# A hybrid attention, scan and expert layer on one core: slot tables by one-hot matmuls, and a reordered beginning and end

## What is computed

```python
h = rms_norm(x, mix_norm_w)
proj = h @ w_in                       # q, k, v, z, xBC, dt, gate_a, gate_s
...                                   # 8-head differential attention, Mamba-2 scan
dt = softplus(dt_raw + dt_bias)       # step sizes of the scan's 32 heads
x = x + (sigmoid(gate_a) * (A @ W_A) + sigmoid(gate_s) * (B @ W_B)) @ w_out
tok = rms_norm(x, moe_norm_w)
logits = tok @ router_w + router_b
top_vals, top_idx = top_k(logits, 4)  # of 32 experts
gate = softmax(top_vals)
...                                   # sort token choices by expert, clamped SwiGLU expert, sum with gates
x = x + sigmoid(rms_norm(x, ple_norm_w) @ w_ple_gate) * (p @ w_ple_proj)
y = rms_norm(x, final_norm_w)
```

## Time and profile before

| | |
|---|---|
| median of three runs | 2371.75 us (2371.46 to 2371.77) |
| the profiled execution | 2371.01 us, its span 2369.3 us |
| TensorE busy | 2126.9 us, 90% of the span |
| VectorE, ScalarE, GpSimd busy | 70%, 53%, 9% |
| mean granted TensorE clock | 0.957 of full speed |
| moved by DMA | 527.68 MB, mean 223 GB/s |
| expert loop | from 1089 to 2268 us |

### The profile page before, as it was taken

The page is one execution under the profiler, slowest core; times in us unless marked ns, Lnnn a source line. Parts: engine busy times, 40 slices in busy tenths (PEclk is TensorE's granted clock), DMA queues, the critical chain, the costliest instruction groups (busy, mean ns, idle before and its releaser), DMA issues.

```text
span 2369.3 us, 30053 instructions
## 1 busy us (share of the span) xinstructions
PE 2126.9 (90%) x9452; PEld 1634.0 (69%) x9452; DVE 1649.7 (70%) x1797; ACT 1248.5 (53%) x1419; POOL 202.5 (9%) x141
## 2 busy tenths in 40 slices
PE   4999799879769999955999999999999999999967
PEld 3777677768645555434877878778778787787746
DVE  4676756668451111135999999999999999999955
ACT  3444243332310010013787777777877777787744
POOL 0000000101000000021021110111101111110020
PEclk9999899989879999967999999999999999999989
DMA  3225222112023222065999999999999999999672
GB/s 97 77 55 195 55 80 63 51 38 71 18 92 104 78 55 62 29 231 181 356 364 389 367 369 382 366 385 374 359 387 370 370 383 366 384 370 365 242 244 87
DMA packets 244019, 527.68 MB, mean 223 GB/s; under 512 B 19830, under 2 KB 127942, under 8 KB 243974
## 3 DMA queue, kind: packets, MB, share of 16 engines
q1 hardware_dynamic: 228688, 481.73, 56.4%
q0 software_dynamic: 7424, 25.19, 3.0%
q10 hardware_dynamic: 7862, 20.19, 2.1%
HBM read 497.55 MB, written 29.49 MB: 222 GB/s over the span
## 4 chain that ended last, share of the span: by engine, by line
PE 70%; DVE 14%; issue 8%; ACT 4%; DMA 2%; ACTq 0%; SPq 0%; DVEq 0%; POOL 0%; POOLq 0%
PE psum L1621 66%; DVE h_lo L1491 4%; ACT h_hi L941 1%; DVE w_lo L1486 1%; PE psum L1901 1%; DVE arena L1506 1%; DVE arena L1189 1%; DVE arena L1509 1%; DVE arena L1516 1%; DVE residual L1564 1%; PE psum L1788 1%; PE psum L1741 1%; DMA arena<-in_final_norm_w 1%; PE psum L1628 1%; DMA arena<-in_lambda_k 0%
## 5 line engine op out<-in xcount | busy, mean ns | idle before, releaser
L1491 DVE TENSOR_TENSOR h_lo<-arena,h_hi 128x1024 fp32r<-128x1024 f32 x768 | 912.0, 1222 | 90.8 <-ACT h_hi L941 54.2
L941 ACT ACTIVATE h_hi<-arena 128x1024 fp32r<-128x1024 f32 x768 | 801.0, 1059 | 219.4 <-PE psum L1621 200.2
L1621 PE MATMUL psum<-h_hi,w_hi 128*128 128x512 f32 x2176 | 870.1, 400 | 20.2 <-DVE h_lo L1491 12.9
L1621 PE MATMUL psum<-h_hi,w_lo 128*128 128x512 f32 x2176 | 850.2, 391 | 0.0
L1621 PE MATMUL psum<-h_lo,w_hi 128*128 128x512 f32 x2176 | 850.2, 391 | 0.0
L1621 PEld LDWEIGHTS psum<-h_hi,w_hi 128*128 128x128 f32 x2176 | 410.9, 189 | 124.7 <-DVE h_lo L1491 26.0
L1621 PEld LDWEIGHTS psum<-h_hi,w_lo 128*128 128x128 f32 x2176 | 410.1, 188 | 87.4
L1621 PEld LDWEIGHTS psum<-h_lo,w_hi 128*128 128x128 f32 x2176 | 411.0, 189 | 84.9 <-issue 3.8
L1621 PE MATMUL psum<-arena 128*128 128x512 f32 (+7 forms) x1232 | 358.3, 459 | 39.5 <-DVE arena L1383 13.4
L1621 PEld LDWEIGHTS psum<-arena 128*128 128x128 f32 (+1 forms) x1232 | 188.4, 198 | 196.4 <-issue 153.8
L1055 DVE TENSOR_TENSOR w_lo<-arena,w_hi 128x1024 fp32r<-128x1024 f32 x80 | 100.5, 1257 | 131.1 <-ACT w_hi L744 130.9
(11 more groups left out here) (264 smaller groups left out, 1547.3 us busy)
## 6 DMA issues: line engine op xcount, KB each, us to landing
arena<-in_w_up SPq DMA_DIRECT2D x512, 512.0 KB, 7.3
arena<-in_w_down SPq DMA_DIRECT2D x256, 512.0 KB, 6.3
arena<-in_w_in SPq DMA_DIRECT2D x80, 512.0 KB, 3.9
y_dram<-arena ACTq DMA_DIRECT2D x32, 512.0 KB, 8.4
arena<-in_w_ssd_branch SPq DMA_DIRECT2D x8, 1024.0 KB, 5.6
y_dram<-arena SPq DMA_DIRECT2D x1, 7680.0 KB, 23.1
arena<-in_w_attn_branch SPq DMA_DIRECT2D x8, 512.0 KB, 3.7
arena<-in_w_out SPq DMA_DIRECT2D x2, 2048.0 KB, 13.3
```

Source lines behind the costliest of these rows:

```text
L941: act.activation(piece_hi[slot], rows, ACT.Copy).then_inc(piece_hi_ready, 1)
L1491: dve.tensor_tensor(piece_lo[slot], rows, piece_hi[slot].bitcast(F32), ALU.subtract).then_inc(piece_lo_ready, 1)
L1621: return pe.matmul(o, l, r, start=start, stop=stop)
```

## The change

1. **Beginning.** The mix norm weights are loaded whole, broadcast over partitions, behind x's first tile, and multiplied in with the scaling (as the router's norm does); the three norm vectors leave the parameter loads, twelve of which remain. The turned tile stays in PSUM, even and odd tiles in two pairs of banks, and both halves are split from there. ScalarE makes a dummy Sqrt before its first Square. The parameters are turned behind the dt projection, the bias loads are issued behind the split of the first two units.
2. **dt steps.** The dt result is turned behind head 0's q unit; `ask_dt` stands before VectorE's split of the third unit and `finish_dt` behind it, ScalarE's Exp calls behind its own part of that split.
3. **Biases.** Their split stands behind VectorE's part of the last head and before its `take_output`; the six stores stand behind ScalarE's last head.
4. **Slot tables.** The scatter, the DRAM table, its reload and its turn are gone. A row number is taken apart in block and place; for each choice VectorE writes a one-hot of its place (128 wide) and, 47 wide each, the token number and the gate at its block. Sixteen matmuls sum them to both tables. The first two gathers read their tokens straight from the table. The control numbers (`ended`, `owner`, `control`) stand behind the tables.
5. **End.** p and its projection go to buffers that come free earlier and are loaded ahead of the norm weights, TensorE waits for them alone, the final weights are loaded once the norm weights have landed. `add_ple` of a tile stands before `end_tile` of the one before.

```diff
+                if t == 0:
+                    sp.dma_start(mix_w, mix_norm_w[0].partition_broadcast(P)).then_inc(mix_w_landed, 16)
...
-            sp.wait_ge(slots_stored, 16 * TT * TOPK)
-            sp.dma_start(slot_rows[0:BLOCKS], slots_dram.rearrange("(b s) two -> b s two", s=P)
-                         ).then_inc(slot_rows_landed, 16)
...
-            sp.dma_start(ple_w, ple_norm_w[0].partition_broadcast(P)).then_inc(ple_in_landed, 16)
+            sp.dma_start(p_sb, p_d.rearrange("(t p) n -> p t n", p=P)).then_inc(ple_in_landed, 16)
+            for k in range(2):
+                sp.dma_start(w_pp[k], w_ple_proj[0, k * P:(k + 1) * P, :]).then_inc(ple_in_landed, 16)
             wait_down_lo(sp, EXPERTS - 1, DOWN_PIECES - 1)
...
-            sp.dma_start(p_sb, p_d.rearrange("(t p) n -> p t n", p=P)).then_inc(ple_in_landed, 16)
-            sp.dma_start(w_pp, w_ple_proj[0].rearrange("(k p) n -> p k n", p=P)).then_inc(ple_in_landed, 16)
-            sp.dma_start(final_w, final_norm_w.partition_broadcast(P)).then_inc(ple_in_landed, 16)
+            sp.dma_start(ple_w, ple_norm_w[0].partition_broadcast(P)).then_inc(ple_w_landed, 16)
+            sp.wait_ge(ple_w_landed, 16)
+            sp.dma_start(final_w, final_norm_w.partition_broadcast(P)).then_inc(ple_w_landed, 16)
...
-            pool.wait_ge(slots_zeroed, 16)
-            pool.wait_ge(slots_ready, 1)
-            for j in range(TT * TOPK):
-                pool.indirect_dma_start(slots_dram, bass.IndirectOffsetOnAxis(rows_u[:, j:j + 1], 0),
-                                        slot_info[:, j, :], None).then_inc(slots_stored, 16)
+            pool.wait_ge(logits_read, TT)
+            pool.iota(iota_slot, [[1, P]], base=0, channel_multiplier=0,
+                      allow_small_or_imprecise_dtypes=True).then_inc(iota_ready, 1)
             def fetch(b):
                 wait(pool, xg_landed, 16 * b)
-                pool.tensor_copy(block_token[:], slot_token[:, ds(b, 1)]).then_inc(block_token_ready, 1)
-                pool.wait_ge(block_token_ready, b + 1)
-                wait(pool, x_turned, b)
+                if isinstance(b, int) and b < 2:
+                    wait(pool, x_turned, b)
+                    token = slot_token[:, b:b + 1]
+                else:
+                    pool.tensor_copy(block_token[:], slot_token[:, ds(b, 1)]).then_inc(block_token_ready, 1)
+                    pool.wait_ge(block_token_ready, b - 1)
+                    wait(pool, x_turned, b)
+                    token = block_token[:]
                 pool.sem_inc(gather_cleared, 1)
-                pool.indirect_dma_start(xg, None, h2_dram, bass.IndirectOffsetOnAxis(block_token[:], 0)
+                pool.indirect_dma_start(xg, None, h2_dram, bass.IndirectOffsetOnAxis(token, 0)
...
-            for src in (mix_norm_w[0], moe_norm_w[0], ple_norm_w[0], ssd_norm_w[0], da_head_norm_w[0], conv_b[0]):
+            for src in (ssd_norm_w[0], da_head_norm_w[0], conv_b[0]):
...
+            own.mark(act.activation(small[:, 0:1], eps[:], ACT.Sqrt))
+            def split_h(t):
+                act.wait_ge(xn_turned, t + 1)
+                act.activation(h_hi[:, :, t * P:(t + 1) * P],
+                               psum[:, (4 - 2 * (t % 2)) * 512:(6 - 2 * (t % 2)) * 512].rearrange("p (k t) -> p k t", t=P),
+                               ACT.Copy).then_inc(h_hi_ready, 1)
...
+            for t in range(TT):
+                root_mean(0, t, xs[:, t, :], lambda: act.wait_ge(x_landed[t], 16), D, square_dump)
+                if t:
+                    split_h(t - 1)
+            split_h(TT - 1)
+            act.wait_ge(w_dt_landed, 16)
+            act.activation(wdt_hi[:], w_dt, ACT.Copy).then_inc(wdt_split, 1)
+            split(Unit(0))
+            split(Unit(1))
+            act.dma_start(bias_src[:, 0:512], b_up[0].rearrange("e n -> (e n)").rearrange("(p n) -> p n", p=P)
+                          ).then_inc(biases_landed, 16)
...
+                if first:
+                    act.wait_ge(lam_asked, 1)
+                    act.activation(lam[:, 2:4], lam[:, 0:2], ACT.Exp).then_inc(lam_exp_ready, 1)
+                    own.mark(act.activation(byhead[:, 1, :], byhead[:, 1, :], ACT.Exp))
+                    act.wait_ge(dt_exp_asked, 1)
+                    act.activation(dt_work[:, 2, :], dt_work[:, 1, :], ACT.Exp).then_inc(dt_exp_ready, 1)
...
+            act.wait_ge(bias_parts_ready, 1)
+            for i in range(3):
+                act.dma_start(bup_dram[i].rearrange("(p n) -> p n", p=P), bias_part[:, i, 0:512]
+                              ).then_inc(bias_stored, 16)
...
+                landed, weights = ((mix_w_landed, mix_w), (moe_w_landed, moe_w), (ple_w_landed, ple_w))[stage]
+                dve.wait_ge(landed, 16)
+                dve.scalar_tensor_tensor(out=buf[t % 2], in0=xs[:, t, :], scalar=stat[:, n, 0:1],
+                                         in1=weights, op0=ALU.mult, op1=ALU.mult).then_inc(xn_ready, 1)
...
+            def split_h(t):
+                dve.wait_ge(h_hi_ready, t + 1)
+                cols = slice(t * P, (t + 1) * P)
+                dve.tensor_tensor(h_lo[:, :, cols],
+                                  psum[:, (4 - 2 * (t % 2)) * 512:(6 - 2 * (t % 2)) * 512].rearrange("p (k t) -> p k t", t=P),
+                                  h_hi[:, :, cols].bitcast(F32), ALU.subtract).then_inc(h_lo_ready, 1)
+            for t in range(TT):
+                normalize(0, t, xn)
+                if t:
+                    split_h(t - 1)
+            split_h(TT - 1)
+            dve.wait_ge(wdt_split, 1)
+            dve.tensor_tensor(wdt_lo[:], w_dt, wdt_hi[:].bitcast(F32), ALU.subtract).then_inc(wdt_split, 1)
+            split(Unit(0))
+            split(Unit(1))
+            dve.wait_ge(dt_projected, 1)
+            dve.tensor_copy(dtT, bank(6)[0:SH]).then_inc(dtt_copied, 1)
...
-            attention(0)
+            attention(0, first=True)
...
             attention(HEADS - 1)
+            dve.wait_ge(biases_landed, 32)
+            own.then(dve.tensor_copy(bias_part[:, 0, :], bias_src))
+            own.then(dve.tensor_tensor(bias_rest, bias_src, bias_part[:, 0, :], ALU.subtract))
+            own.then(dve.tensor_copy(bias_part[:, 1, :], bias_rest))
+            own.then(dve.tensor_tensor(bias_rest, bias_rest, bias_part[:, 1, :], ALU.subtract))
+            dve.tensor_copy(bias_part[:, 2, :], bias_rest).then_inc(bias_parts_ready, 1)
...
+            dve.wait_ge(top_exp_ready, 1)
+            own.then(dve.tensor_reduce(top_sum[:, 0:TT], top_exp, AX, ALU.add))
+            own.then(dve.reciprocal(top_sum[:, 4:4 + TT], top_sum[:, 0:TT]))
+            own.mark(dve.tensor_tensor(gate_of, top_exp,
+                                       top_sum[:, 4:4 + TT].unsqueeze(2).broadcast_to([P, TT, TOPK]), ALU.mult))
...
+            own.then(dve.tensor_copy(rows_u[:], row_f))
+            own.then(dve.tensor_scalar(slot_u, rows_u[:], P - 1, None, ALU.bitwise_and))
+            own.then(dve.tensor_copy(slot_f, slot_u))
+            own.then(dve.tensor_tensor(block_f, row_f, slot_f, ALU.subtract))
+            by_block = [P, TT * TOPK, BLOCKS]
+            own.then(dve.tensor_tensor(block_hot[:, :, 0, :], iota_block[:].unsqueeze(1).broadcast_to(by_block),
+                                       block_f.unsqueeze(2).broadcast_to(by_block), ALU.is_equal))
+            own.mark(dve.tensor_tensor(block_hot[:, :, 1, :], block_hot[:, :, 0, :],
+                                       gate_of.rearrange("p t k -> p (t k)").unsqueeze(2).broadcast_to(by_block), ALU.mult))
+            own.wait()
+            for t in range(TT):
+                own.mark(dve.tensor_scalar(block_hot[:, t * TOPK:(t + 1) * TOPK, 0, :],
+                                           block_hot[:, t * TOPK:(t + 1) * TOPK, 0, :], token_id[:, t:t + 1], None,
+                                           ALU.mult))
+            for b in range(2):
+                dve.wait_ge(h2_stored[b], 16 * TT // 2)
+            dve.wait_ge(iota_ready, 1)
+            own.wait()
+            for t in range(TT):
+                by_slot = [P, TOPK, P]
+                dve.tensor_tensor(slot_hot[:, t * TOPK:(t + 1) * TOPK, :], iota_slot.unsqueeze(1).broadcast_to(by_slot),
+                                  slot_f[:, t * TOPK:(t + 1) * TOPK].unsqueeze(2).broadcast_to(by_slot), ALU.is_equal
+                                  ).then_inc(slots_ready, 1)
+            dve.wait_ge(slots_summed, 1)
+            own.mark(dve.tensor_copy(slot_token[:], bank(6, BLOCKS)))
+            own.wait()
+            dve.tensor_copy(gate_tab[:], bank(6, BLOCKS, BLOCKS)).then_inc(tables_ready, 1)
...
             add_ple(0)
             ple_split(3)
+            add_ple(1)
+            dve.wait_ge(ple_w_landed, 32)
             end_tile(0)
-            add_ple(1)
+            add_ple(2)
             end_tile(1)
-            add_ple(2)
+            add_ple(3)
             end_tile(2)
-            add_ple(3)
             end_tile(3)
...
```

(44 more changed lines are left out.)

213 lines of the change are left out of this document (74 added, 139 removed).

## The result

| | before | after |
|---|---|---|
| median of the runs shown with the result | 2371.6 us | 2329.4 us (2325.0 to 2331.1) |
| ratio to before, 95% interval | | 0.982 (0.981 to 0.983) |
| profiled execution, its span | 2371.0, 2369.3 us | 2325.0, 2323.2 us |
| mean granted clock of the span | 0.957 | 0.962 |

The forecast was 2330.9 us. Five more runs of the changed kernel, beside other runs of before, gave 2329.7 (2324.5 to 2331.8), ratio 0.982 (0.981 to 0.984). Runs of one kernel lie up to 7 us apart, so a difference of medians is good to some 2 us; where less is asked, the place in the trace decides. The runs of before beside each group of experiments had medians of 2369.5 to 2372.3 us, so experiments of different groups (1 to 4, 5 to 8, 9 to 11, 12) can differ by some 2 us for that reason too.

A forecast was written before the change was run, and what follows sets the result against it. TensorE, busy 90% of the span, was taken as the bound, so only its standstills could give time. -14.5 - 19.4 - 2.8 - 4.1 = -40.8 us from the median 2371.75 gave 2330.9 us, range 2324 to 2339.

The forecast's parts named there:

- Beginning: Start to head 0's scores: shorter ScalarE queue, earlier dt projection, clock level held; -14.5 us, bounds -11.7 to -16.
- Bias split: Five VectorE steps and six ScalarE issues fit in waits at the last head: 0; without that cover 3.75 us.
- Router: Row numbers to the first gather's landing, tables summed by matmuls instead of scatters: -19.4 us, bounds -13.5 to -22.5.
- rival (a): Router: 62 further columns add 3.3 us to the passes and the gather takes 8 us; 2336 us, chance 0.11.
- The row that I set against it: Profile row of 512-column passes at 0.43 us each, said to leave no room for a weight load beside the columns.
- Rival (e): Router: the first expert waits for something else, VectorE's low halves or weights; 2350 us, chance 0.03.
- Loop: Expert 0's first matmul to expert 31's last keeps its length, within 2 us of 1179; costed at nothing.
- End: Loads behind the last expert: turns of p and the adds come earlier, -2.8 us, bounds -1.5 and -4.
- rival (c): End gives nothing before its last steps, gathers or gate-weight split being late anyway; 2333.7 us, chance 0.07.
- Tail: Last output steps: the last tile's sum no longer waits for the output of tile 2; -4.1 us.
- Rival (b): Beginning gains 2.8 us less: ScalarE's issues still end at 9.3, first unit starts slow; 2333.7 us, chance 0.10.
- Rival (d): Granted clock falls in the expert loop, at 150 us of it 2360 us; chance 0.03, 0.02 of it slower than before.

The follow-up runs named there:

- experiment 1: Changed kernel with the router's slot tables made as before, by sixteen GpSimd scatters, reload and turns: 2347.6 us.
- experiment 3: Changed kernel with the last output steps in the old order, output step of a tile before the sum of the next: 2333.8 us.
- experiment 4: Changed kernel with p and its projection loaded behind the norm weights and TensorE waiting for all five loads, as before: 2331.8 us.
- experiment 10: Changed kernel without ScalarE's dummy Sqrt ahead of the first Square: 2329.3 us.
- experiment 2: Changed kernel with the two bias loads issued ahead of the first Square again: 2331.6 us.
- experiment 12: Kernel of experiment 9 with the twelve small parameter loads issued by SyncE behind x, dt weights and two units, not by ScalarE: 2321.8 us, ratio 0.979.
- experiment 11: Changed kernel with VectorE's five bias steps behind the copy of the last head's output instead of ahead: 2331.7 us.
- experiment 8: Changed kernel with thirteen of the sixteen table matmuls 376 columns wide instead of 94: 2332.3 us.
- experiment 7: Changed kernel with the control numbers made beside the table sums instead of behind the tables: 2332.1 us.
- experiment 5: Changed kernel run again unaltered, for its spread: 2329.7 us.
- experiment 6: Changed kernel with tables made tile by tile and four low halves of the gate weights ahead of the copy of p: 2326.8 us, ratio 0.981.
- experiment 9: Changed kernel with tables made tile by tile, and p and its projection issued ahead of the gate weights: 2325.5 us, ratio 0.981.

## Why the prediction was right, and where its steps were off

**Beginning**, -14.5 taken, -16.2 at head 0's scores, -15.5 at the row numbers; the medians leave it 17.6 (41.9 less the 17.9, 4.2 and 2.2 of experiments 1, 3 and 4). The steps named came as laid out: the removed second table load (experiment 10), the 4 us that VectorE's order holds tile 2, the level held from the dt projection on, the dt turns behind unit 0. The cover of the dt step chain held: it ended at 46.9 and kT was copied by 47.5, 4 us ahead of the scores. The term mis-sized is ScalarE's queue. I kept the last issues at what they took before, ending near 8.0; they ended at 6.93 (experiment 2: an issue behind fewer loads is 0.5, not 1.4 to 2.2). The mix weights ahead of x cost nothing at that start; at the earlier start of experiment 12 x's tiles are what is late.

**Bias split**, 0, and 3.75 without its cover: 0 (the shift is the same 15.5 us on both sides of it) and 3.65 (experiment 11).

**Router**, -19.4 taken, -20.9 in the trace, -20.15 and -17.9 by undoing it. The tables stood 12.9 us behind the start of the row numbers' sum: block tables 0.94 each for 0.98, passes 7.11 for 7.1, so rival (a) was out by the first trace. The row that I set against it held, but the clock beside it was 1.00 and not 0.50 (experiment 8): a column costs half as much there. The sentence of the Trainium skill on weight loads (TensorE: Matmul & The Clock Gate) stands there under The mechanism; the traces disagree with it, as these passes take what their columns take, with nothing for the load. The term mis-sized is the gather, 4.29 for 6.0. I had seen that the control numbers put off the next weights, and took only half of it: the gather is then alone, and beside them it is 7.34 (experiment 7). Rival (e) didn't come.

**Loop**, 0: 1179.2 to 1178.6, but this is luck, from two parts that nearly cancel. TensorE ran expert 0's first matmuls at the 1.2 GHz level for 2.7 us, before 5.7, and its first two rounds took 69.2 us for 71.4; the last expert gave 1.7 back (experiment 5).

**End**, -2.8 taken for the loads, -4.5 to the first add in the trace, 4.3 by undoing it in the trace and 2.2 in the medians. p was turned 7.1 us behind the last matmul, where I had 8 to 9; the other traces with this order of loads have 7.7 to 10.0. Of rival (c) a part is true: the fourth add waited 0.43 us for its gather, and with the low halves earlier the gathers are the bound (experiment 6). **Tail**, -4.1 taken, -4.2 measured and 4.2 by undoing it.

**Rival (b)** had the issues end late: they ended early. **Rival (d)**: the loop kept its clock at 1.00.

**The spread.** Those first two rounds are of two kinds: 69.2 to 69.4 us in six of the fourteen traces (both of the changed kernel, experiments 1, 2, 7, 8) and 70.8 to 71.7 in the other eight, and what differs is how soon the clock rises in expert 0. The stretch where it begins, in the changed kernel and in experiment 3:

```profile
1050.00:1060.00 10.00, 7.63 (x28) 5.95 (x27) 4.10 (x4) 4.43 (x5) 1.98 (x2) 0.72 0.65 217
```

```profile
1050.00:1060.00 10.00, 7.59 (x21) 6.03 (x22) 3.31 (x3) 2.21 (x3) 1.27 (x2) 0.50 0.67 234
```

Seven matmuls fewer in the same busy time. That is 2.4 us of the 7 that runs of one kernel differ by, and no step of mine had it as a chance. The quick runs also have the higher clock: of the nine runs of the changed kernel the three under 2327 us have a mean granted clock of 0.962 or 0.963, the six others 0.959 to 0.961. What stays open: why the clock rises early in some executions, the rest of the spread, and why the medians of experiments 1, 4, 10 and 11 show 1.6 to 2.2 us less than their traces. The changed kernel was traced twice, in executions of 2325.0 and 2326.1 us, both with the short rounds; those near 2330 have no trace.

## What to carry to other kernels

Ahead of a first instruction, count an engine's DMA issues at what they cost in a short queue as well as in the long one, and ask whether they must stand there at all: moving twelve small loads to another queue gave 2.9 us at the dt projection (experiment 12). A gather that the path waits for should be issued before whatever frees space for bulk loads; 1.8 us of small steps in the right place were worth 3. At the end, taking two loads out of what TensorE waits for was worth 4.3 us in the trace (experiment 4), but swapping the order of loads that are all waited for changed the name of the wait and not its end (experiment 9).

## What the runs showed of the hardware

GpSimd's indirect DMA took 0.93 to 0.98 us to issue in the expert loop and when VectorE was idle. Beside VectorE's low halves, which follow each other every 1.15 us and whose two operands both lie in SBUF, it took what was left of the running one and 0.88 us more: 1.98 when it began 0.04 us into it (changed kernel, the first gather of y), 1.32 at 0.71 (experiment 10), 1.16 at 0.86 (experiment 6), 1.06 at 0.97 (experiment 4). So it waits once, for the step that is running, and then goes on beside the next. The Trainium skill (SBUF — State Buffer, Who interferes with whom) says that a VectorE step with two SBUF inputs contends with a GpSimd instruction that reads SBUF, over ports that the two share under an exclusive lock, and the trace agrees.

Passes of 94 columns held the granted clock at 0.50 for all of 7.1 us; with 376 columns it rose to 1.00 inside the stretch (experiment 8), and the narrow passes behind it took 0.14 us each for 0.22. A pass of these f32 matmuls costs 1.67 ns a column at clock 0.50 and 0.83 at 1.00, with a floor for narrow ones; an fp32r matmul of 512 columns takes 0.43 and 0.23 us, half of that a column. Whoever reads a duration of TensorE from a trace has to read the type and the granted clock beside it.
